# Four tiles of the second mixer and of the query projection begun from x, the root multiplied into their results

## What is computed

```python
def rmsnorm(x, g):
    return x * rsqrt(mean(x * x, -1) + EPS) * g

# first block: feed-forward, attention with a gated mix, feed-forward
x = x + 0.5 * rmsnorm(swiglu(rmsnorm(x, g_pre_ffn1), w_gu1, w_down1), g_post_ffn1)
z = rmsnorm(x, g_pre_mix) @ w_in
...
x = x + rmsnorm(merged @ w_out, g_post_mix)
x = x + 0.5 * rmsnorm(swiglu(rmsnorm(x, g_pre_ffn2), w_gu2, w_down2), g_post_ffn2)
# second block
h = concatenate([meta, x])
proj = rmsnorm_2(h, g_mix) @ w_in_2          # rgx tiles, hyena tiles, gates
...
h = h + merged @ w_out_2
n = rmsnorm_2(h, g_ffn)
q = n @ peer_wq                              # query projection, then keys, top 16 and experts
h = h + peer(n, ...)
out = rmsnorm_2(h, g_final)[:, N_META:]
```

## Time and profile before

| | us |
|---|---|
| median of three runs | 1957.2 |
| the three runs | 1957.2, 1952.1, 1962.52 |
| the profiled execution | 1954.4 |
| its span, first to last instruction | 1952.3 |
| TensorE busy | 1856.4 (95%) |
| VectorE, ScalarE, POOL busy | 1080.6, 926.6, 941.0 |
| granted TensorE clock, mean | 0.976 |

### The profile page before, as it was taken

One profiled execution on the slowest core, in us unless ns is written; L12 is line 12 of the kernel. 1 busy time (PEld: TensorE's weight loads), 2 busy tenths in 40 slices (PEclk: granted clock), 3 DMA queues, 4 the chain that ended last, 5 costly groups with the idle time before them and its releaser, 6 DMA issues.

```text
span 1952.3 us, 39493 instructions
## 1 busy us (share of the span) xinstructions
PE 1856.4 (95%) x14418; PEld 1771.3 (91%) x14418; DVE 1080.6 (55%) x1951; ACT 926.6 (47%) x1523; POOL 941.0 (48%) x379
## 2 busy tenths in 40 slices
PE   8999999999989999999999998779999999999998
PEld 8999987787889999977998997668999999999998
DVE  4665553474425665648564997995544344344344
ACT  4344532454454445576444454994334444444443
POOL 3566574732546665610016689007874444444442
PEclk8999999999999998999998999999999999999998
DMA  7555443521435554443553554003555555555553
GB/s 252 168 187 188 147 140 102 190 88 53 141 107 184 183 184 139 142 140 98 169 185 134 172 183 140 22 0 133 179 169 187 183 187 188 184 183 186 188 184 107
DMA packets 83887, 297.40 MB, mean 152 GB/s; under 512 B 10244, under 2 KB 12709, under 8 KB 83558
## 3 DMA queue, kind: packets, MB, share of 16 engines
q1 hardware_dynamic: 81376, 290.49, 45.0%
q10 hardware_dynamic: 2438, 5.89, 0.8%
HBM read 295.30 MB, written 1.05 MB: 152 GB/s over the span
## 4 chain that ended last, share of the span: by engine, by line
PE 79%; POOL 7%; issue 4%; DVE 4%; ACT 4%; ACTq 0%; POOLq 0%; DMA 0%; DVEq 0%; SPq 0%
PE ps L1540 22%; PE ps L1541 21%; PE ps L1542 21%; POOL ring_lo L445 7%; ACT aux L873 2%; PE ps L1747 2%; PE ps L1570 2%; PE ps L2039 1%; PE ps L1589 1%; PE ps L1590 1%; PE ps L1921 1%; PE ps L1712 1%; PE ps L1530 1%; DVE peer_split L1471 1%; PE ps L1599 1%
## 5 line engine op out<-in xcount | busy, mean ns | idle before, releaser
L1542 PE MATMUL ps<-h_hi,ring_lo 128*128 128x256 f32 (+1 forms) x2432 | 684.2, 281 | 0.0
L445 POOL TENSOR_TENSOR ring_lo<-ring,peer_split 128x1024 fp32r<-128x1024 f32 x170 | 428.3, 2520 | 423.9 <-ACT peer_split L553 418.8
L1542 PEld LDWEIGHTS ps<-h_hi,ring_lo 128*128 128x128 f32 x2432 | 462.1, 190 | 0.0
L445 POOL TENSOR_TENSOR ring_lo<-ring,main_hi 128x1024 fp32r<-128x1024 f32 x113 | 285.2, 2524 | 243.2 <-ACT main_hi L553 236.6
L445 POOL TENSOR_TENSOR ring_lo<-ring,more_hi 128x1024 fp32r<-128x1024 f32 x87 | 226.3, 2601 | 320.1 <-ACT more_hi L553 316.3
L553 ACT ACTIVATE peer_split<-ring 128x1024 fp32r<-128x1024 f32 x256 | 270.6, 1057 | 209.1 <-PE ps L1542 208.9
L1540 PE MATMUL ps<-h_hi,peer_split 128*128 128x256 f32 x1024 | 288.2, 281 | 10.8 <-POOL ring_lo L445 10.8
L1540 PE MATMUL ps<-peer_split 128*128 128x256 f32 x1024 | 289.4, 283 | 9.2 <-DVE peer_split L1471 6.6
L1541 PE MATMUL ps<-h_lo,peer_split 128*128 128x256 f32 x1024 | 288.7, 282 | 0.0
L1541 PE MATMUL ps<-peer_split 128*128 128x256 f32 x1024 | 287.8, 281 | 0.0
L1542 PE MATMUL ps<-peer_split,ring_lo 128*128 128x256 f32 x1024 | 286.7, 280 | 0.0
(11 more groups left out here) (328 smaller groups left out, 3930.1 us busy)
## 6 DMA issues: line engine op xcount, KB each, us to landing
ring<-in_stream SPq DMA_DIRECT2D x550, 512.0 KB, 3.3
arena<-in_decay ACTq DMA_DIRECT2D x1, 1536.0 KB
x<-in_x SPq DMA_DIRECT2D x4, 256.0 KB, 5.3
arena<-in_keys ACTq DMA_DIRECT2D x1, 1024.0 KB, 5.6
out<-h SPq DMA_DIRECT2D x4, 256.0 KB, 2.4
aux<-in_dft ACTq DMA_DIRECT2D x1, 816.0 KB
aux<-in_idft ACTq DMA_DIRECT2D x1, 768.0 KB
arena<-in_mask ACTq DMA_DIRECT2D x1, 768.0 KB, 5.8
```

What stands on the lines that cost most here:

```text
L445: nc.gpsimd.tensor_tensor(ring_lo[:, c % NS, :], ring[:, c % NS, :], hi_part(c).bitcast(F32), ALU.subtract).then_inc(lo_pool, 1)
L1542: return M(out, w_lo, parts[0], start=False, stop=stop, skip_group_check=True)
```

## The change

At rgx and at wq the first four tiles (`EARLY`) are made from x times the gain, without the root. For this ScalarE writes an early high part of x, followed by its square, and VectorE an early low part (`early_low`). VectorE then multiplies the root into the four results (`scale_early` at rgx, in place in the bank; at wq the multiplication replaces ScalarE's copy). The square sums move into the opening. The true h is still made for the other tiles and for what follows, and tile 4 waits for its low parts one by one. `opening` can start single tiles some steps late, so that a bank may come free.

With it go: `residual` writes its product into the banks of the sums and not into h, and waits for the copies in pairs; the banks of qk and wq are given out in another order; two waits for `gy_ready` are dropped; some `hi_to` and `root(2)` change places; and at three places six f32 products of the identity with itself (`warm_up`) stand in front of an opening, their result unused. `rstd_out` is 272 wide instead of 256.

Left out here: the declarations of the new semaphores and of the wider `rstd_out`, with the slices that follow from it.

```diff
@@ -48,6 +48,7 @@
 NW = 3
+EARLY = 4
 CW = 1024
@@ -168,6 +169,8 @@
     merged2_parts = over("merged2_parts", "arena", RT * (2 * L + T), [P, 2, KT, T])
+    early_rgx = over("early_rgx_hi", "arena", 6400, [P, KT, L]), over("early_rgx_lo", "arena", 6400 + KT * L, [P, KT, L])
+    early_wq = over("early_wq_hi", "arena", 17664, [P, KT, T]), over("early_wq_lo", "arena", 17664 + KT * T, [P, KT, T])
     gg_parts = over("gg_parts", "arena", RT * (3 * L + 2 * T), [P, 2, RT, T])
@@ -374,7 +378,7 @@
-    return ps[:, n - 3 if n in (4, 5) else (3, 0, 4, 5)[n % 4], :]
+    return ps[:, (4, 5, 0, 1, 2, 3)[n] if n < 6 else (4, 5, 0, 3)[(n - 6) % 4], :]
@@ -390,7 +394,7 @@
-    return ps[:, (1, 3)[n] if n < 2 else 4 + n % 2, :]
+    return ps[:, (4, 5, 1, 3)[n] if n < 4 else 4 + n % 2, :]
@@ -631,20 +635,19 @@
     gained(1, "g_post_ffn1", True)
+    hi_to(START["qk"] + 4)
     for k in range(KT):
         scaled_hi(2, k, "g_pre_mix")
-        if k == 3:
-            hi_to(START["qk"] + 4)
+    root(2, T)
     hi_to(START["qk"] + 5)
-    root(2, T)
             act_e.wait_ge(lam_sum, 1)
-            A(small[:, 4:6], ps[:, 2, 0:2], ACT.Exp).then_inc(lam_exp, 1)
+            A(small[:, 4:6], ps[:, 3, 0:2], ACT.Exp).then_inc(lam_exp, 1)
             act_e.wait_ge(lam_e, 1)
@@ -741,19 +744,22 @@
     gained(5, "g_post_ffn2", True)
+    hi_to(START["rgx"] + 4)
     act_e.wait_ge(loaded_const, 16 * N_CONST)
         act_e.wait_ge(x_ready, 2 * KT + k + 1)
+        A(early_rgx[0][:, k, :], x[:, k, :], ACT.Copy, scale=col(NORMS[6], k)).then_inc(early_hi, 1)
         squared_in(6, k, x[:, k, :], L)
-        if k == 3:
-            hi_to(START["rgx"] + 4)
     root(6, L)
+    hi_to(START["rgx"] + 5)
     input_hi(0, L)
-    hi_to(START["rgx"] + 5)
     for n in range(RT):
-        act_e.wait_ge(chunk_done, START["rgx"] + n + 1)
+        if n < EARLY:
+            act_e.wait_ge(early_scaled, n + 1)
+        else:
+            act_e.wait_ge(chunk_done, START["rgx"] + n + 1)
         for d in range(2):
@@ -827,11 +833,12 @@
         act_e.wait_ge(x_ready, 3 * KT + k + 1)
+        A(early_wq[0][:, k, :], real(x, k), ACT.Copy, scale=col(NORMS[7], k)).then_inc(early_hi, 1)
         squared_in(7, k, real(x, k))
     act_e.dma_start(keys, keys_d).then_inc(loaded_keys, 16)
+    hi_to(START["wq"] + 4)
     root(7, T)
     input_hi(KT)
-    hi_to(START["wq"] + 4)
@@ -840,8 +847,9 @@
     for n in range(16):
-        act_e.wait_ge(chunk_done, START["wq"] + n + 1)
-        A(pq[:, n, :], wq_bank(n)[:, 0:T], ACT.Copy).then_inc(pq_copied, 1)
+        if n >= EARLY:
+            act_e.wait_ge(chunk_done, START["wq"] + n + 1)
+            A(pq[:, n, :], wq_bank(n)[:, 0:T], ACT.Copy).then_inc(pq_copied, 1)
         if n and n % 4 == 0:
@@ -955,13 +965,18 @@
             if k < KT:
-                dve.wait_ge(gy_ready, n // 2 * KT + k + 1)
-                V.tensor_tensor(h[:, k, 0:T], h[:, k, 0:T], rstd(T), ALU.mult).then_inc(dve_step, 1)
+                dve.wait_ge(gy_ready, n // 2 * KT + (k | 1) + 1)
+                V.tensor_tensor(acc(k), h[:, k, 0:T], rstd(T), ALU.mult).then_inc(dve_step, 1)
                 steps[0] += 1
                 dve.wait_ge(dve_step, steps[0] - (k < KT))
-                V.tensor_tensor(real(x, k - 1), real(x, k - 1), h[:, k - 1, 0:T], ALU.add).then_inc(x_ready, 1)
+                V.tensor_tensor(real(x, k - 1), real(x, k - 1), acc(k - 1), ALU.add).then_inc(x_ready, 1)
+    def early_low(seen, k, parts, src, name):
+        dve.wait_ge(early_hi, seen + k + 1)
+        V.scalar_tensor_tensor(parts[1][:, k, :], src, col(name, k), parts[0][:, k, :].bitcast(F32), ALU.mult, ALU.subtract).then_inc(early_lo, 1)
@@ -1228,12 +1243,22 @@
     residual(5)
+    for k in range(KT):
+        early_low(0, k, early_rgx, x[:, k, :], NORMS[6])
     norm_in(6, NORMS[6], lambda k: x[:, k, :], lambda k: h[:, k, :], L)
+    def scale_early(n):
+        dve.wait_ge(chunk_done, START["rgx"] + n + 1)
+        V.tensor_tensor(in2_bank(n)[:, 0:L], in2_bank(n)[:, 0:L], rstd_out[:, :], ALU.mult).then_inc(early_scaled, 1)
     input_lo(3, L)
+    scale_early(0)
+    scale_early(1)
     for n in range(RT):
+        if n + 2 < EARLY:
+            scale_early(n + 2)
         dve.wait_ge(rg_tap, 2 * n + 2)
@@ -1375,9 +1400,16 @@
         V.tensor_tensor(real(x, n), real(x, n), ps[:, n % 4, 0:T], ALU.add).then_inc(x_ready, 1)
+        if n:
+            early_low(KT, n - 1, early_wq, real(x, n - 1), NORMS[7])
     dve.wait_ge(x_ready, 32)
+    early_low(KT, KT - 1, early_wq, real(x, KT - 1), NORMS[7])
     norm_in(7, NORMS[7], lambda k: real(x, k), lambda k: real(h, k), T)
-    input_lo(4)
+    for n in range(EARLY):
+        if n == 2:
+            input_lo(4)
+        dve.wait_ge(chunk_done, START["wq"] + n + 1)
+        V.tensor_tensor(pq[:, n, :], wq_bank(n)[:, 0:T], rstd_out[:, 0:T], ALU.mult).then_inc(early_scaled, 1)
     tiu = ti.bitcast(U32)
@@ -1578,20 +1610,30 @@
-    def opening(first, outs, begins, parts, hi_sem, lo_sem, seen, n=None):
-        for k in range(KT):
-            pe.wait_ge(hi_sem, seen + k + 1)
+    def warm_up(n):
+        for _ in range(n):
+            M(ps[:, 6, T:T + P], ident, ident, start=True, stop=True)
+    def opening(first, outs, begins, parts, hi_sem, lo_sem, seen, n=None, late=(0, 0, 0, 0), w=T, x_seen=None):
+        for step in range(KT + max(late)):
+            if step < KT:
+                pe.wait_ge(hi_sem, seen + step + 1)
             for m, out in enumerate(outs):
-                c = first + m
+                c, k = first + m, step - late[m]
+                if not 0 <= k < KT:
+                    continue
                 if k == 0:
                     low(c)
+                if k == 0 and m == 3 and x_seen:
+                    pe.wait_ge(x_ready, x_seen)
                 M(out, hi_part(c)[:, k * P:(k + 1) * P], parts(k)[0], start=(k == 0 and begins[m]), stop=False, skip_group_check=True)
                 M(out, ring_lo[:, c % NS, k * P:(k + 1) * P], parts(k)[0], start=False, stop=False, skip_group_check=True)
-            if n is not None and k:
-                sum_of(n, k - 1)
-        if n is not None:
-            sum_of(n, KT - 1)
+            if n is not None and 1 <= step <= KT:
+                sum_of(n, step - 1, w)
+        if n is not None and not max(late):
+            sum_of(n, KT - 1, w)
         for pair in range(0, len(outs), 2):
@@ -1600,7 +1642,7 @@
     if n is not None and pair == 0:
-        spread_rstd(n)
+        spread_rstd(n, w)
@@ -1655,7 +1697,6 @@
     else:
-        pe.wait_ge(gy_ready, 2 * KT)
         opening(base, [ps[:, 4 + m // 2, m % 2 * T:(m % 2 + 1) * T] for m in range(4)], (True, False, True, False), h_real, h_hi, h_lo, 2 * KT, 4)
@@ -1679,6 +1720,7 @@
     spread_rstd(1)
+    warm_up(6)
@@ -1713,16 +1755,15 @@
-    pe.wait_ge(gy_ready, KT)
-    opening(START["qk"], [qk_bank(m)[:, 0:T] for m in range(4)], (True,) * 4, h_real, h_hi, h_lo, KT, 2)
+    opening(START["qk"], [qk_bank(m)[:, 0:T] for m in range(4)], (True,) * 4, h_real, h_hi, h_lo, KT, 2, (0, 0, 2, 4))
     pe.wait_ge(lam_prod, 2)
-    M(ps[:, 2, 0:2], ones, small[:, 0:2], start=True, stop=True).then_inc(lam_sum, 1)
+    M(ps[:, 3, 0:2], ones, small[:, 0:2], start=True, stop=True).then_inc(lam_sum, 1)
     turned = 0
         elif n > 5:
-            pe.wait_ge(qk_ready, n - 3 if n in (6, 7) or n > 9 else n - 7)
+            pe.wait_ge(qk_ready, n - 5 if n < 9 else n - 3)
         tile(START["qk"] + n, qk_bank(n)[:, 0:T], h_real).then_inc(chunk_done, 1)
@@ -1869,19 +1910,17 @@
     spread_rstd(3)
+    warm_up(6)
     ffn(1, START["ffn2"])
     spread_rstd(5)
-    for k in range(KT):
-        sum_of(6, k, L)
-    pe.wait_ge(x_ready, 3 * KT)
-    spread_rstd(6, L)
-    opening(START["rgx"], [in2_bank(m)[:, 0:L] for m in range(4)], (True,) * 4, h_all, h_hi, h_lo, 3 * KT)
+    warm_up(6)
+    opening(START["rgx"], [in2_bank(m)[:, 0:L] for m in range(4)], (True,) * 4, lambda k: (early_rgx[0][:, k, :], early_rgx[1][:, k, :]),
+            early_hi, early_lo, 0, 6, (0, 0, 2, 4), L)
     for n in range(4, RT):
             pe.wait_ge(rg_conv, n - 5)
-        tile(START["rgx"] + n, in2_bank(n)[:, 0:L], h_all).then_inc(chunk_done, 1)
+        tile(START["rgx"] + n, in2_bank(n)[:, 0:L], h_all, (h_lo, 3 * KT) if n == EARLY else None).then_inc(chunk_done, 1)
     for n in range(12):
@@ -1969,14 +2008,13 @@
-    for k in range(KT):
-        sum_of(7, k)
-    pe.wait_ge(x_ready, 32)
-    spread_rstd(7)
     def key_scores(n):
         g = n // 4
-        pe.wait_ge(pq_copied, n + 1)
+        if n < EARLY:
+            pe.wait_ge(early_scaled, EARLY + n + 1)
+        else:
+            pe.wait_ge(pq_copied, n - EARLY + 1)
         if n == 0:
@@ -1986,11 +2024,16 @@
-    opening(START["wq"], [wq_bank(m)[:, 0:T] for m in range(4)], (True,) * 4, h_real, h_hi, h_lo, 4 * KT)
+    pe.wait_ge(x_ready, 3 * KT + 6)
```

(9 more changed lines are left out.)

15 lines of the change are left out of this document (9 added, 6 removed).

## The result

| kernel | median us | runs | to before |
|---|---|---|---|
| before | 1956.5 | 20 | |
| changed | 1961.2 | 20 | 1.0029 [1.0018, 1.0039] |
| changed, once more beside the experiments (before: 1954.8) | 1960.0 | 12 | 1.0027 [1.0014, 1.0040] |

The forecast was 1.5 us faster, 1955.0. The medians differ by 4.7 us the other way, the ratio by 0.29%, which is 5.7 us. The time lies inside the range and within 0.5% of before, but the sign is wrong. The profiled execution of the changed kernel took 1962.0 us (span 1960.1). Its chain, beside the earlier trace rows, tells little: the share of "issue" (time in which the engine waited for nothing that the profile shows) is larger, and no line of the four seams stands in it with more than 1%.

A forecast was written before the change was run, and what follows sets the result against it. TensorE, with 79% of the chain, was taken as the bound, losing time only where it stands still or runs at half clock. 2.2 + 1.2 + 2.1 - 4.0 = 1.5 us gained, from 1956.5 to 1955.0; range 1944 to 1963.

The forecast's parts named there:

- four seams: Places the diff touches where TensorE stands or runs at half clock: ffn1 to qk, out1 to ffn2, ffn2 to rgx, out2 to wq.
- seams 1 to 3: ffn1 to qk, out1 to ffn2, ffn2 to rgx: gains of 2.2, 1.2 and 2.1 us.
- seam 4: out2 to wq: longer ScalarE loop, late POOL splits, sums inside the opening; loss 4.0 us (1.5 to 10).
- Seams 1 and 2: ffn1 to qk, gain 2.2 us (1.2 to 2.7); out1 to ffn2, gain 1.2 us (0.2 to 2.1).
- seam 3: ffn2 to rgx: opening 11.8 us earlier, waits before tiles 4 and 6 give back 5; gain 2.1 us (0.5 to 8).
- Behind each seam TensorE streams, so what a seam gains reaches the end: After all four places, past the routing too: gains carry through to the end of the kernel.
- Warm-ups: Products before openings at qk and ffn2 raise the clock 2.1 and some 2.3 us sooner; at rgx hidden.
- The port: VectorE's second SBUF input and GpSimd share a locked port pair; residual with PSUM scratch avoids it, 0.75 us instead of 2.87.
- Rival B: At wq POOL gets the lock before `input_lo`: up to 8 us more, 1963; chance 0.08.
- A: Faster rival: the two waits at rgx and the late opening at wq don't form; 1945, chance 0.14.
- C: Rival: warm-up products don't bring the clock back sooner; 1957.8, chance 0.12.
- the forecast's: Main case: two waits at rgx, late opening at wq, earlier clock at qk and ffn2; 1955.0, chance 0.66.

The follow-up runs named there:

- no_wq_packed: Changed kernel with the query projection as before and `stat` packed, so small, arena and aux stand at before's addresses: 1950.9 us, ratio 0.9981.
- after_packed: Complete changed kernel with `stat` packed (2 x 24), so small, arena and aux are back at the addresses of before: 1955.5 us, ratio 1.0004.
- sums_first: after_packed with wq's eight square sums ahead of its opening, root spread after the third step, `input_lo` ahead of all scalings: 1946.6 us, ratio 0.9970.
- no_warm: no_wq_packed with all three groups of warm-up products taken out: 1965.6 us, ratio 1.0062.

## Why the prediction was wrong

Against before on the same chip (1954.8) the changed kernel lost 5.3 us. By the runs: 6.3 for the query projection, 4.3 for the 64 bytes, and what is left, -5.3, for seams 1 to 3. The last is a remainder and so takes up every error of the 4.3. A second account stays at the addresses of before and on one chip: no_wq_packed is 4.3 us faster than before (seams 1 to 3), and after_packed is 4.6 us slower than no_wq_packed (seam 4). The whole change at these addresses stands at 1.0004 [0.9987, 1.0022], and the forecast of 0.9992 lies inside. So without the 64 bytes no clear loss is left; the forecast gain isn't shown either.

- **Seams 1 to 3**: forecast 5.5 gained, measured 5.3 (1954.8 + 4.3 - 1953.8) or 4.3 (no_wq_packed). Seams 1 and 2 alone 4.2 (1954.8 + 4.3 - 1954.9; forecast 3.4), seam 3 the other 1.2 (forecast 2.1), each within some 1.5 us of scatter and the 2 us or so by which the 4.3 can be off.
- **The step that failed first is a term that the sum puts at nothing.** "Behind each seam TensorE streams, so what a seam gains reaches the end" takes the pace of those streams as unchanged, and 2.2 + 1.2 + 2.1 - 4.0 has no term for it. That `rstd_out` is 272 wide stands in the section on the change, but no row of before could have shown its price. The runs showed a stream of 118.5 ns a matmul in place of 117.8 and 4.3 us for it, three times the forecast gain.
- **Seam 4**: the right waits at the right places (2.95 for 3.2, tile 4 at 1051.1), and wrong by the clock. The text let the opening run at half clock only at its start; it was so for 10 to 20 us of it. Forecast 4.0, measured 6.3 (4.6 between after_packed and no_wq_packed), inside the bounds of 1.5 to 10. The term that was mis-sized is the opening's length. Its end, "1046.1 to 1047.0", was met in the first profile (last product at 1047.9, the part in front being 1.4 late), but tiles 0 to 3 took 3.3 and 4.7 us longer in the repetition and in after_packed. That the sums inside hold the clock down fits the profiles of this seam (10.3 to 20.5 us with them, 6.8 in sums_first without), but it isn't shown as the whole cause: sums_first changed the order with them, and openings of qk with the same kind of sums inside came back after 3.4 to 6.8 us in most profiles. What makes one stretch long and the next short stays open.
- **Seam 3**: the opening began early as forecast, and the two waits formed. ScalarE's first early high part came as it should behind the split of rgx+4, and tile 6 was held by POOL. The changed kernel gained 1.4 us here (44.9 to 43.5), after_packed 3.0: the order is the same, but the lower level falls on tile 6 in the one (804.3 to 807.7) and on tile 4 in the other (802.4 to 805.9), in front of the wait for POOL, which takes it up.
- **Warm-ups**: "earlier by the 2.1 us that the warm-ups fill" had the right sign and the wrong size. In before these openings come back to full clock by themselves in 6.8 us; in the new order without products they may not (27.3 at rgx; at qk 17.0 in one profile and 6.8 in the other). The comparison was made with the kernel before and should have been made with the new order. Why the opening of qk comes back by itself in before and in no_warm, with the same kind of sums inside, stays open.
- **The port** (the paragraph "Page and row"): the new residual's last two adds take 0.75 us, the figure that the prediction gave (it stands in none of its rows), instead of the 2.87 of the earlier trace rows; the early low parts at wq, with two inputs in SBUF, take 2.30 beside POOL and 0.48 without it. Rival B didn't form: POOL's split of wq+5 came after `input_lo` had begun and was the one that waited, 4.12 us. The timeline of the changed kernel, VectorE and then POOL:

```profile
776.57 0.75 DVE L974 TENSOR_TENSOR x<-x,ps 128x256 f32<-128x256 f32 x2
...
1021.40 0.48 DVE L979 SCALAR_TENSOR_TENSOR early_wq_lo<-x,cols,early_wq_hi 128x256 fp32r<-128x256 f32 x1
1022.99 2.30 DVE L979 SCALAR_TENSOR_TENSOR early_wq_lo<-x,cols,early_wq_hi 128x256 fp32r<-128x256 f32 x1 [0.78 <-ACT early_wq_hi L836]
...
1022.63 2.38 POOL L449 TENSOR_TENSOR ring_lo<-ring,more_hi 128x1024 fp32r<-128x1024 f32 x1 [185.75 <-ACT more_hi L557]
1051.43 4.12 POOL L449 TENSOR_TENSOR ring_lo<-ring,main_hi 128x1024 fp32r<-128x1024 f32 x1 [16.35 <-ACT main_hi L557]
```

- POOL began its splits at 1022.63, 3.25 later than in the earlier trace rows; by 1.4 of it the program was late anyway, and 1.9 are the loop's (forecast 2.0).
- **Rivals**: A (no waits) is refuted by the rows above, C (products without effect) by no_warm. Of the four cases the forecast's came nearest, with its waits at their places; the loss came from outside all four. That the time is still inside the range is owed to the range's width, not to a case that foresaw it.

## What to carry to other kernels

When a time doesn't fit its waits, compare the pace of a stretch that the change doesn't touch, and keep the addresses of all buffers when one is widened: 64 and 32 bytes cost 0.6% and 1.4% of TensorE's pace here. Openings that were cut up by one-column products stayed at the lower clock for up to 27 us here, though not in every profile; try such sums in front, where the engine waits anyway, and filler products that run up to the first matmul. One profile of a kernel doesn't tell how long such a stretch lasts: repeat it. An early start is worth what the next wait leaves of it: the same early query projection cost 6.3 us with its sums inside and gained 4.5 with them in front.

## What the runs showed of the hardware

- TensorE's mean time from matmul to matmul (256 columns, fp32r) changes with the place in SBUF of `small`, `arena` and `aux`, which hold its high weight parts among others: 117.8 ns at shifts of 0 and 96 bytes, 118.5 at 64 and 128, 119.4 at 32 (17.20 us for 144). All ten profiles at shift 0 had the first value and all six at 64 the second, whatever else was changed. Which buffer or operand it is, and by what rule, wasn't tried.
- Most of the scatter between runs of one kernel goes with the granted clock: within the fifteen kernels with several runs beside the experiments (156 runs) the time falls by 1.7 us for each 0.001 of mean granted clock (0.9 to 2.3 by kernel).
